# Three stages of a two-block kernel in a new order: the start, the join between output projection and swiglu, and the last stage of attention

## The chip, the cores and the metric

The kernel runs on one core of a Trainium2 chip. The metric is the device time of one execution in microseconds, the median of the runs. TensorE (PE) multiplies; VectorE (DVE), ScalarE (ACT) and GpSimd (POOL) work element by element; SyncE (SP) issues DMAs. Each engine works through its own queue in order and waits at semaphores for the others.

## What is computed

Two transformer blocks on a sequence of 1024 tokens of width 1024, with a context of 256 tokens for the first block. The first block modulates a normed input by vectors made from `c` and `c_ctx` (the "ada" product), mixes tokens (chunked MLP and gated linear attention), and closes with a swiglu. The second has an LRU branch, banded attention, and again a swiglu:

```python
mod = jnp.split((jax.nn.silu(c) @ w_ada[l] + b_ada[l])[:, None, :], N_MOD, axis=-1)
h_lat = _modulate(_rmsnorm(x, norm1_g[l]), sh1, sc1)
h_ctx = _modulate(_rmsnorm(ctx, norm1_g[l]), sh1c, sc1c)
...
x = x + g1 * mix_l
x = x + g2 * _swiglu(_modulate(_rmsnorm(x, norm2_g[l]), sh2, sc2), w_ffn_in[l], w_ffn_out[l])
...
merged = gates[:, :, 0] * y_a + gates[:, :, 1] * y_b
x = x + merged @ w_out[l]
xn2 = rmsnorm(x, norm_ffn_g[l])
gu = xn2 @ w_ffn_in[l]
x = x + (jax.nn.silu(ff_gate) * ff_up) @ w_ffn_out[l]
```

## The kernel before

All data stand transposed: 8 tiles of 128 features, tokens along the free axis, in a context part (256) and two halves (512 each), "half 0" and "half 1". To keep fp32 accuracy every operand is split into a high part (ACT, a copy to fp32r: `s_xh`, `s_wh`) and a low part (DVE, the difference: `s_xl`, `s_wl`), and a product is three matmuls: high by high (L290), low by high (L291), high by low (L292). A *job* is one 128-column tile of a weight by one half: 24 matmuls over 8 tiles k. `products_pe` runs several jobs side by side, k outermost, so that with two jobs each k takes 6 matmuls; `mids` are calls put in ahead of a k.

Weights go through a ring: raw tiles by SP into two buffers `WS` (512 KB each), high parts into four places `WH`, low parts into `WL`. A raw tile is loaded when the tile two before it has its low part, and a place in `WH` is free when the product four tiles before is done. `weights_act`, `weights_dve`, `weights_sp` advance the ring to a given tile, and where they stand in a queue decides when.

The order of each engine is written out by hand, stage by stage, in functions `sp_`, `pe_`, `act_`, `dve_`, `pool_`. The steps that recur:

- An rms norm of a half: ACT squares 8 tiles, DVE or POOL adds them (L1500, L1493), PE sums the columns (`sums_pe`, L1508: 4 matmuls of one column), ACT takes the root, DVE the reciprocal and a diagonal `s_dia` (L1513), PE spreads it to all partitions (`spread_pe`, L1545), DVE scales each tile (L1591), ACT takes the high, DVE the low part.
- Stage 0 (L442 on): the ada product (L570) of 8 row tiles into four banks, the squares and sums of the context and both halves, ACT's copy of the four bank rows (`s_mrow`, L618), 16 transposes of them (L596), the modulated context and half 0. Stage 1 begins with `firsts`: four jobs (al, k0, k1, k2) by context, half 0 and half 1, and half 1 is modulated in between, on DVE after the first jobs' low part (L855).
- `residual_stage("wo", ...)` (L1768): pairs of jobs (p, h) for p in 0 to 3 and h in 0, 1, in that order. After each, DVE adds the gained result to x (tiles `s_lq`, four buffers, loaded by SP) into `s_res`, ACT squares, POOL adds. The norm of half 0 stands in the last pair, that of half 1 at the head of the swiglu.
- `swiglu` (L1877): four plain pairs of jobs (two tiles by two halves; the column sums of half 1 ahead of k = 3, the spread ahead of k = 6 of the first). Then 20 tiles, each as seven products of 12 matmuls (L2126 to L2128) instead of eight: P1, P2, P6, P5, P7, P4, P3. Their inputs are sums of quarters of the normed input: T1, T2, T3 and T4, made once on DVE and ACT (T4 takes the place of half 1's upper tiles); their weights are folded sums S1 to S4 of raw quarters on DVE (L2353 to L2360), with high parts on ACT (L2266) and low parts on DVE (L2367).
- Stage 6 (L3010): 32 units of attention with 16 fill jobs beside them. The last eight multiply half 0 by `wo2` and store the result. Stage 7 (L3300) loads it and x2 back (`s_res`, `s_lq`), adds them to half 0's result, and multiplies half 1 by the same weights in four pairs (`wo2b`), with the norm of half 0 in them.

## Time and profile before

| | us |
|---|---|
| median of 3 runs | 3408.72 |
| lowest and highest | 3406.57 and 3416.22 |
| profiled execution | 3411.13 |
| its span (first to last instruction) | 3409.8 |
| busy: PE, weight loads, DVE, ACT, POOL | 3261.6, 2651.7, 1928.6, 1379.7, 384.0 |

The granted clock of PE was 0.984 of full speed on average. A row of the timeline gives the start and the duration in us, the engine, the line, the operation, what it writes and reads, and in brackets how long the engine had been idle and what released it. Full-speed 128x512 matmuls overlap, so their spacing tells the rate, not their duration.

### The profile page before, as it was taken

Reading aid. Unit: us, or ns where it says so; the run is one execution under the profiler, and the core shown is the slowest. Engines: PE = TensorE matmul, PEld = TensorE weight load, DVE = VectorE, ACT = ScalarE, POOL = GpSimd, SP = SyncE. Lnnn points to the kernel's source line nnn. Section 1 sums busy time; section 2 is a strip of 40 time slices with the busy share of each in tenths; the row PEclk is TensorE's granted clock in tenths of the full one; section 3 lists DMA queues with packets and bytes.
Section 4 is the critical chain, followed back from the end, with each engine's and each line's share of the span. In section 5 each row is a group of like instructions: output and inputs, shape, how many; then the busy total and the mean of one; then the engine's idle time right before and its main releaser. Section 6 shows DMA issues by size and latency. Waiting matters only on the chain. (4 is left out here: it accounts for less than half of the span.)

```text
span 3409.8 us, 39604 instructions
## 1 busy us (share of the span) xinstructions
PE 3261.6 (96%) x14862; PEld 2651.7 (78%) x14862; DVE 1928.6 (57%) x3098; ACT 1379.7 (40%) x2325; POOL 384.0 (11%) x605
## 2 busy tenths in 40 slices
PE   6999999999999999999999999998888799999998
PEld 3888888878888778888888888877556588888886
DVE  4474433456334387777445454664676587777443
ACT  4593222244333243333233355554575343333221
POOL 0121100002100300000011101111211200001011
PEclk8999999999999999999999999999999899999999
DMA  5366444346543323334852434445744523335752
GB/s 220 107 206 197 134 126 135 124 148 224 190 156 99 126 90 118 105 118 150 254 176 81 164 108 148 134 147 164 163 93 105 185 90 121 112 111 170 240 182 75
DMA packets 228045, 494.14 MB, mean 145 GB/s; under 512 B 21520, under 2 KB 84624, under 8 KB 226320
## 3 DMA queue, kind: packets, MB, share of 16 engines
q1 hardware_dynamic: 147728, 302.30, 28.0%
q0 software_dynamic: 80128, 189.30, 17.0%
q8 instruction: 120, 1.97, 0.2%
q14 instruction: 69, 0.57, 0.1%
HBM read 353.63 MB, written 137.89 MB: 144 GB/s over the span
## 5 line engine op out<-in xcount | busy, mean ns | idle before, releaser
L290 PE MATMUL p<-s_xh,s_wh 128*128 128x512 f32 x2256 | 901.6, 400 | 32.9 <-DVE s_tmp L401 12.3
L291 PE MATMUL p<-s_xl,s_wh 128*128 128x512 f32 x2256 | 885.3, 392 | 0.0
L292 PE MATMUL p<-s_xh,s_wl 128*128 128x512 f32 x2256 | 885.2, 392 | 0.0
L290 PEld LDWEIGHTS p<-s_xh,s_wh 128*128 128x128 f32 x2256 | 428.6, 190 | 127.3 <-issue 22.6
L292 PEld LDWEIGHTS p<-s_xh,s_wl 128*128 128x128 f32 x2256 | 427.5, 190 | 91.2
L291 PEld LDWEIGHTS p<-s_xl,s_wh 128*128 128x128 f32 x2256 | 428.4, 190 | 88.8 <-issue 1.7
L2126 PE MATMUL p<-s_xh,s_wh 128*128 128x512 f32 x1152 | 449.5, 390 | 2.1 <-DVE s_xl L2233 1.1
L2128 PE MATMUL p<-s_xh,s_wl 128*128 128x512 f32 x1152 | 448.2, 389 | 0.0
L2127 PE MATMUL p<-s_xl,s_wh 128*128 128x512 f32 x1152 | 448.2, 389 | 0.0
L250 DVE TENSOR_TENSOR s_wl<-s_ws,s_wh 128x1024 fp32r<-128x1024 f32 x157 | 195.3, 1256 | 232.9 <-ACT s_wh L242 232.6
L2126 PEld LDWEIGHTS p<-s_xh,s_wh 128*128 128x128 f32 x1152 | 216.3, 188 | 48.8 <-issue 4.2
L389 ACT ACTIVATE s_tmp<-p 128x512 f32<-128x512 f32 (+1 forms) x125 | 74.3, 594 | 441.0 <-PE p L292 441.0
L2127 PEld LDWEIGHTS p<-s_xl,s_wh 128*128 128x128 f32 x1152 | 216.3, 188 | 45.1 <-issue 0.5
L2128 PEld LDWEIGHTS p<-s_xh,s_wl 128*128 128x128 f32 x1152 | 216.3, 188 | 45.1
L242 ACT ACTIVATE s_wh<-s_ws 128x1024 fp32r<-128x1024 f32 x157 | 162.7, 1049 | 76.5 <-PE p L292 35.3
L2266 ACT ACTIVATE s_wh<-s_ws 128x512 fp32r<-128x512 f32 x148 | 91.9, 625 | 146.7 <-PE p L2128 112.1
L2266 ACT ACTIVATE s_wh<-s_qb 128x512 fp32r<-128x512 f32 x140 | 87.3, 625 | 119.3 <-PE p L2128 111.7
L2477 POOL DMA_DIRECT2D d_h<-s_fhl x80 | 42.6, 533 | 756.6 <-DVE s_fhl L2372 724.0
L2367 DVE TENSOR_TENSOR s_wl<-s_ws,s_wh 128x512 fp32r<-128x512 f32 x148 | 106.4, 731 | 32.5 <-ACT s_wh L2266 32.3
L2367 DVE TENSOR_TENSOR s_wl<-s_qb,s_wh 128x512 fp32r<-128x512 f32 x140 | 100.1, 724 | 37.5 <-ACT s_wh L2266 37.3
L2272 ACT ACTIVATE s_fhl<-s_rb 128x512 fp32r<-128x512 f32 x80 | 50.7, 634 | 141.2 <-DVE s_rb L2410 135.0
L1493 POOL TENSOR_TENSOR s_acc<-s_acc,s_tmp 128x512 f32<-128x512 f32 x49 | 63.7, 1301 | 354.5 <-ACT s_tmp L1486 354.3
(381 smaller groups left out, 5102.4 us busy)
## 6 DMA issues: line engine op xcount, KB each, us to landing
d_h<-s_fhl POOLq DMA_DIRECT2D x80, 512.0 KB, 3.2
s_ws<-i_Wf SPq DMA_DIRECT2D x48, 512.0 KB, 4.3
s_qb<-i_Wf SPq DMA_DIRECT2D x40, 512.0 KB, 4.0
s_qb<-i_Wf SPq DMA_DIRECT2D x80, 256.0 KB, 3.1
s_ws<-i_Wf SPq DMA_DIRECT2D x80, 256.0 KB, 2.9
s_aw<-i_adaT SPq DMA_DIRECT2D x32, 512.0 KB, 3.6
s_xh<-d_h POOLq DMA_DIRECT2D x16, 1024.0 KB, 12.1
s_xl<-d_h POOLq DMA_DIRECT2D x16, 1024.0 KB, 14.8
```

Source lines behind the costliest of these rows:

```text
L242: ac.activation(WH[:, i % NW, 0:n], WS[:, i % NS, 0:n], ACT.Copy).then_inc(*w_hi.up())
L250: dv.tensor_tensor(WL[:, i % NW, 0:n], WS[:, i % NS, 0:n], WH[:, i % NW, 0:n].bitcast(F), ALU.subtract).then_inc(*w_lo.up())
L290: pe.matmul(o, wh, H[:, k, c:c + n], start=(k == 0), stop=False)
L291: pe.matmul(o, wh, L[:, k, c:c + n], start=False, stop=False)
L292: last = pe.matmul(o, wl, H[:, k, c:c + n], start=False, stop=(k == 7))
L389: ac.activation(o, ps, ACT.Copy, scale=p.scale).then_inc(*evA.up())
L1493: po.tensor_tensor(a, a, TMP[:, s.slot, :], ALU.add).then_inc(*sumP.up())
L2126: pe.matmul(o, wh[:, c], H[:, k, :], start=(start and k == 0), stop=False)
L2127: pe.matmul(o, wh[:, c], L[:, k, :], start=False, stop=False)
L2128: x = pe.matmul(o, wl[:, c], H[:, k, :], start=False, stop=(stop and k == 3))
L2266: ac.activation(half_tile(u.slot)[0], u.src, ACT.Copy).then_inc(*u_hi.up())
L2367: dv.tensor_tensor(l, u.src, h.bitcast(F), ALU.subtract).then_inc(*u_lo.up())
```

## The change

1. **Stage 0 and the first products.** Loads: `cc` first, then the ada tiles, with the context, weight tiles 0 to 3 (2 and 3 raw in `ACC` and `RB`) and x in half tiles of 256 KB between them. Squares go to space in `TMP` and to ada tiles that are done with; ACT squares half 0 and half 1 whole, DVE adds the context's and half 0's, POOL half 1's. All four weight tiles are split before the ada product ends. Two bank rows are copied by ACT, two by DVE. The column sums and spreads of both halves stand inside `firsts`, which moved into stage 0; half 1's spread is copied to `s_rb`. The context keys are stored from `ACC`.
2. **`residual_stage`.** The order of pairs is (0,0), (0,1), (1,0), (1,1), (2,0), (3,0), (2,1), (3,1). Half 0's column sum stands ahead of k = 5 of (2,1), its spread ahead of k = 0 of (3,1). In the norm, the results of (2,1) are taken before tile 1, and two weight tiles split before tile 4.
3. **`swiglu`.** Half 1's column sum and spread stand ahead of k = 0 and k = 2 of the second plain pair. The first of the 20 tiles runs P1, P2, P6, P5, P7, P3, P4, and the low parts of its weights are made ahead of those of T2 and T3 where their products come first. T3's sums stand in `RB` instead of `ACC`.
4. **Stages 6 and 7.** Four of the eight `wo2` results are kept in SBUF (`PART`) rather than stored. x2 has eight buffers (`X2`), loaded with the four stored results after the last score product, ahead of further weight tiles. Half 0's column sum and spread stand ahead of k = 2 and k = 6 of the third pair.

```diff
+        def sp_():
+            sp.dma_start(sc2[:], D["cc"]).then_inc(*cc_in.up())
+            for k in range(8):
+                sp.dma_start(AD[:, k, :], D["ada"][k]).then_inc(*ad_in[k].up())
+                if k == 0:
+                    sp.dma_start(XC[:], D["ctxT"]).then_inc(*xc_in.up())
...
+                elif 2 <= k < 6:
+                    weights_sp(k - 1)
+                elif k == 6:
+                    x_sp(0, range(4))
...
+        def pe_():
+            for k in range(8):
+                ada_pe(k)
+                if k == 2:
+                    columns_pe("c")
+                if k == 4:
+                    spread_pe("c")
+            columns_pe(0)
...
+            products_pe(firsts[0], {3: lambda: spread_pe(0)})
+            products_pe(firsts[1], {1: lambda: columns_pe(1), 3: lambda: spread_pe(1)})
+            products_pe(firsts[2])
...
+            for k in range(8):
+                high_act("c", k)
+                if k < 6:
+                    square_act(1, 2 + k)
+            for k in range(2):
+                high_act(0, k)
+            ACW.wait_ge(*w_lo.at(3))
+            for g, p in enumerate(firsts[0][1:]):
+                ACW.wait_ge(*p.mm)
+                ac.activation(ACC[:, 256 * g:256 * g + 256], B[p.bank][:, 0:256], ACT.Copy).then_inc(*evA.up())
+            al_act(0)
+            root_act(1)
...
+            modulated_dve("c", {1: lambda: inverse_dve(0)})
+            modulated_dve(0, {5: lambda: inverse_dve(1)})
+            al_dve(0)
+            modulated_dve(1)
...
+        def pool_():
+            for k in range(1, 8):
+                POW.wait_ge(*squares.at(16 + k + 1))
+                POW.wait_ge(*added1.at(k - 1))
+                po.tensor_tensor(SQ[1][0], SQ[1][0], SQ[1][k], ALU.add).then_inc(*added1.up())
...
-        pairs = plan_pairs(name)
+        pairs = plan_pairs(name, [(0, 0), (0, 1), (1, 0), (1, 1), (2, 0), (3, 0), (2, 1), (3, 1)])
...
-                if p == 3 and h == 1:
-                    products_pe(js, {4: lambda: sums_pe(s0)})
-                    spread_pe(0, DIA[:, 0, :], s0.diag, n0.q[7])
-                else:
-                    products_pe(js)
+                products_pe(js, {5: lambda: sums_pe(s0)} if (p, h) == (2, 1) else {0: lambda: spread_pe(0, DIA[:, 0, :], s0.diag, n0.q[7])} if (p, h) == (3, 1) else None)
...
-                products_pe(e.js, {3: lambda: sums_pe(s1), 6: lambda: spread_pe(1, DIA[:, 1, :], s1.diag, q1[7])} if e is plain[0] else None)
+                products_pe(e.js, {0: lambda: sums_pe(s1), 2: lambda: spread_pe(1, DIA[:, 1, :], s1.diag, q1[7])} if e is plain[1] else None)
...
+        def products_of(p):
+
+            return PRODUCTS if p.n else PRODUCTS[:5] + PRODUCTS[:4:-1]
...
-        items += [("wo2", m, "new first", "plain", dW2, "wo2", 1.0, TC) for m in range(8)]
+        items += [("wo2", m, "new first", "plain", dW2, "wo2", 1.0, TC) for m in range(4)]
+        items += [("wo2", m, "new first", "kept", (PART[:, m, :], sc_mm.at(128)), "wo2", 1.0, TC) for m in range(4, 8)]
...
-            products_pe(pairs[1], {6: lambda: sums_pe(s0)})
-            products_pe(pairs[2], {4: lambda: spread_pe(0, DIA[:, 0, :], s0.diag, n0.q[7])})
+            products_pe(pairs[1])
+            products_pe(pairs[2], {2: lambda: sums_pe(s0), 6: lambda: spread_pe(0, DIA[:, 0, :], s0.diag, n0.q[7])})
```

ACT's queue in the start stage, before: `s_rb`, `s_acc` and `s_tmp` from `s_xc` and `s_res` are squares, `s_rc` the roots, `s_wh` the weights' high parts, `s_mrow` the bank rows.

```order
5 L505 ACTIVATE s_tmp<-s_res 128x512 x10
6 L606 ACT_TABLE_LOAD
7 L606 ACTIVATE s_rc<-p,s_eps 128x2
8 L505 ACTIVATE s_tmp<-s_res 128x512 x4
9 L606 ACTIVATE s_rc<-p,s_eps 128x4 x2
10 L242 ACTIVATE s_wh<-s_ws 128x1024 x2
11 L618 ACTIVATE s_mrow<-p 2x512 x4
12 L242 ACTIVATE s_wh<-s_ws 128x1024 x2
13 L521 ACTIVATE s_ch<-s_tmp,s_modc 128x256 x8
14 L521 ACTIVATE s_xh<-s_tmp,s_mod 128x512 x8
```

The same queue in the change, up to the first context tiles (`s_ch`); the squares now go to `s_ad`.

```order
4 L616 ACTIVATE s_rc<-p,s_eps 128x2
5 L250 ACTIVATE s_wh<-s_ws 128x1024 x2
6 L250 ACTIVATE s_wh<-s_acc 128x1024
7 L250 ACTIVATE s_wh<-s_rb 128x1024
8 L610 ACTIVATE s_ad<-s_res 128x512 x8
9 L640 ACTIVATE s_mrow<-p 2x512 x2
10 L616 ACTIVATE s_rc<-p,s_eps 128x4
11 L610 ACTIVATE s_ad<-s_res 128x512 x2
12 L622 ACTIVATE s_ch<-s_tmp,s_modc 128x256
13 L610 ACTIVATE s_ad<-s_res 128x512
14 L622 ACTIVATE s_ch<-s_tmp,s_modc 128x256
```

The four weight tiles moved ahead of the squares of half 0 and of the bank rows, and squares of half 1 stand between the context tiles.

DVE's queue at the first of the 20 tiles of the first block's swiglu, before, from the last T2 low part: `s_t2l`, `s_t3l` are low parts of T2 and T3, `s_wl` those of the weights, `s_acc` and `s_s` the folded weights, `s_tmp` and `s_fhl` a plain pair's result.

```order
700 L2233 TENSOR_TENSOR s_t2l<-s_lq,s_t2h 128x512 x4
701 L2233 TENSOR_TENSOR s_t3l<-s_acc,s_t3h 128x512 x2
702 L2233 TENSOR_TENSOR s_t3l<-s_s,s_t3h 128x512 x2
703 L2378 TENSOR_TENSOR s_tmp<-p,s_tmp 128x512
704 L2372 TENSOR_TENSOR s_fhl<-s_tmp,s_fhl 128x512
705 L2367 TENSOR_TENSOR s_wl<-s_ws,s_wh 128x512
706 L2353 TENSOR_TENSOR s_acc<-s_ws 128x512
707 L2355 TENSOR_TENSOR s_acc<-s_acc,s_ws 128x512
708 L2367 TENSOR_TENSOR s_wl<-s_ws,s_wh 128x512
709 L2367 TENSOR_TENSOR s_wl<-s_acc,s_wh 128x512
```

And in the change:

```order
703 L2421 TENSOR_TENSOR s_tmp<-p,s_tmp 128x512
704 L2415 TENSOR_TENSOR s_fhl<-s_tmp,s_fhl 128x512
705 L2410 TENSOR_TENSOR s_wl<-s_ws,s_wh 128x512
706 L2395 TENSOR_TENSOR s_acc<-s_ws 128x512
707 L2397 TENSOR_TENSOR s_acc<-s_acc,s_ws 128x512
708 L2410 TENSOR_TENSOR s_wl<-s_ws,s_wh 128x512
709 L2271 TENSOR_TENSOR s_t2l<-s_lq,s_t2h 128x512 x4
710 L2410 TENSOR_TENSOR s_wl<-s_acc,s_wh 128x512 x2
711 L2421 TENSOR_TENSOR s_tmp<-p,s_tmp 128x512
712 L2415 TENSOR_TENSOR s_fhl<-s_tmp,s_fhl 128x512
713 L2271 TENSOR_TENSOR s_t3l<-s_rb,s_t3h 128x512 x2
714 L2271 TENSOR_TENSOR s_t3l<-s_s,s_t3h 128x512 x2
```

The low parts of P1's and P2's weights stand before the eight low parts of T2 and T3, where they stood behind them.

SP's queue at stage 7, before: `s_ws` are weight tiles, `s_lq` x2, `s_res` the stored results (the two alternate eight times).

```order
350 L260 DMA s_ws<-i_Wwo 128x1024 x5
351 L3352 DMA s_lq<-d_x 128x512
352 L3362 DMA s_res<-d_wo 128x512
353 L3352 DMA s_lq<-d_x 128x512
354 L3362 DMA s_res<-d_wo 128x512
```

And in the change (four alternations, then four x2 tiles alone):

```order
351 L269 DMA s_ws<-i_Wwo 128x1024 x3
352 L3397 DMA s_x2half<-d_x 128x512
353 L3406 DMA s_parthalf<-d_wo 128x512
...
360 L3397 DMA s_x2half<-d_x 128x512 x4
361 L269 DMA s_ws<-i_Wwo 128x1024 x2
362 L3397 DMA s_x2half<-d_x 128x512 x8
```

Two of the five weight tiles moved behind the loads of half 0, and those of half 1 stand together.

## Rows read from the trace of the kernel before

**Rows 1.** The page's first part: busy time, share and instructions.
```profile
PE 3261.6 (96%) x14862; PEld 2651.7 (78%) x14862; DVE 1928.6 (57%) x3098; ACT 1379.7 (40%) x2325; POOL 384.0 (11%) x605
```

**Rows 2.** Stretches: busy us, records, granted clock, DMA share, GB/s.
```profile
1300.00:1350.00 50.00, 50.00 (x223) 41.39 (x222) 36.63 (x58) 19.63 (x34) 3.19 (x6) 1.00 0.36 122
1180.00:1190.00 10.00, 7.57 (x26) 5.42 (x25) 5.16 (x8) 3.06 (x5) 0.26 (x1) 0.84 0.00 0
```

**Rows 3.** Timeline of PE at the start: start, duration, operation, idle before.
```profile
7.44 16.81 PE L570 MATMUL p<-s_ad,s_sc 128*2 128x512 f32 x32 [7.44 <-DMA s_ad<-i_ada]
...
40.39 3.60 PE L570 MATMUL p<-s_ad,s_sc 128*2 128x512 f32 x8
...
50.71 0.40 PE L290 MATMUL p<-s_ch,s_wh 128*128 128x256 f32 x1 [3.46 <-DVE s_cl L531]
...
57.27 0.55 PE L290 MATMUL p<-s_ch,s_wh 128*128 128x256 f32 x1 [5.10 <-DVE s_wl L250]
...
81.58 0.76 PE L290 MATMUL p<-s_xh,s_wh 128*128 128x512 f32 x1 [11.32 <-DVE s_al L855]
...
126.57 0.39 PE L292 MATMUL p<-s_xh,s_wl 128*128 128x512 f32 x1
```

**Rows 4.** Timeline at the start: bank rows, turning, first context tile.
```profile
44.02 2.02 ACT L618 ACTIVATE s_mrow<-p 2x512 f32<-2x512 f32 x4 [1.37 <-PE p L570]
...
46.09 1.15 PE L596 MATMUL p<-s_ident,s_mrow 2*128 2x2 f32 x16 [0.20 <-ACT s_mrow L618]
...
49.60 0.89 ACT L521 ACTIVATE s_ch<-s_tmp,s_modc 128x256 fp32r<-128x256 f32 x2
```

**Rows 5.** Timeline of PE at the first block's join.
```profile
1175.58 1.05 PE L1508 MATMUL p<-s_ones,s_acc 128*128 128x1 f32 x8 [1.33 <-POOL s_acc L1493]
...
1187.10 0.47 PE L290 MATMUL p<-s_xh,s_wh 128*128 128x512 f32 x1 [2.43 <-ACT s_xh L1575]
...
1201.66 2.07 PE L1545 MATMUL p<-s_dia,s_ones 128*128 128x512 f32 x2 [3.31 <-DVE s_dia L1513]
...
1240.50 0.47 PE L2126 MATMUL p<-s_xh,s_wh 128*128 128x512 f32 x1 [0.94 <-DVE s_wl L2367]
...
1254.93 0.47 PE L2126 MATMUL p<-s_xh,s_wh 128*128 128x512 f32 x1 [0.55 <-DVE s_xl L2233]
```

**Rows 6.** Timeline of DVE at the same join.
```profile
1203.78 1.41 DVE L2172 SCALAR_TENSOR_TENSOR s_qb<-s_res,s_gs,p 128x512 f32<-128x512 f32 x2 [2.17 <-PE p L1545]
...
1232.86 2.49 DVE L2233 TENSOR_TENSOR s_t2l<-s_lq,s_t2h 128x512 fp32r<-128x512 f32 x4
...
1239.67 0.68 DVE L2367 TENSOR_TENSOR s_wl<-s_ws,s_wh 128x512 fp32r<-128x512 f32 x1
```

**Rows 7.** Timeline of DVE and POOL, an addition of squares beside low parts.
```profile
1187.58 0.74 DVE L1598 SCALAR_TENSOR_TENSOR s_xl<-s_tmp,s_mod,s_xh 128x512 fp32r<-128x512 f32 x1
...
1189.74 1.28 POOL L1493 TENSOR_TENSOR s_acc<-s_acc,s_tmp 128x512 f32<-128x512 f32 x1 [13.72 <-ACT s_tmp L1486]
...
1190.22 1.35 DVE L1598 SCALAR_TENSOR_TENSOR s_xl<-s_tmp,s_mod,s_xh 128x512 fp32r<-128x512 f32 x1
```

**Rows 8.** Timeline of PE at the second block's join.
```profile
2643.90 0.50 PE L290 MATMUL p<-s_xh,s_wh 128*128 128x512 f32 x1
...
2677.78 1.87 PE L1508 MATMUL p<-s_ones,s_acc 128*128 128x1 f32 x8 [9.07 <-DVE s_acc L1500]
...
2713.88 0.77 PE L290 MATMUL p<-s_xh,s_wh 128*128 128x512 f32 x1 [6.78 <-DVE s_wl L250]
...
2725.72 1.86 PE L1508 MATMUL p<-s_ones,s_acc 128*128 128x1 f32 x8 [6.16 <-POOL s_acc L1493]
...
2783.92 0.47 PE L2126 MATMUL p<-s_xh,s_wh 128*128 128x512 f32 x1 [0.54 <-DVE s_xl L2233]
```

**Rows 9.** Timeline of DVE at the second block's join.
```profile
2734.05 1.41 DVE L2172 SCALAR_TENSOR_TENSOR s_qb<-s_res,s_vec,p 128x512 f32<-128x512 f32 x2 [5.23 <-PE p L1545]
...
2768.67 0.68 DVE L2367 TENSOR_TENSOR s_wl<-s_ws,s_wh 128x512 fp32r<-128x512 f32 x1
```

More of the change, by code:

```diff
@@ L378, in fill_act @@
             ac.activation(VF[p.vq][:, 0:p.n], ps, ACT.Copy).then_inc(*evA.up())
+            return
+        if p.kind == "kept":
+            out, free = p.dst
+            ACW.wait_ge(*free)
+            ac.activation(out, ps, ACT.Copy).then_inc(*evA.up())
             return
@@ L555, in stage0 @@
[L555 removed]
+        column_bank, spread_bank = {"c": 6, 0: 6, 1: 3}, {"c": 4, 0: 5, 1: 3}
         scale_of = {"c": GS[:, 8:16], 0: GS[:, 0:8], 1: GS[:, 0:8]}
         shift_of = {"c": MODC, 0: MOD, 1: MOD}
[L559 to L564 removed]
@@ new lines, in ada_pe, with columns_pe @@
+        def ada_pe(k):
+            PEW.wait_ge(*silu.at(1))
+            PEW.wait_ge(*ad_in[k].at(1))
+            for c in range(4):
+                last = pe.matmul(B[c][0:2, :], sc2[:, k, :], AD[:, k, c * 512:c * 512 + 512], start=(k == 0), stop=(k == 7))
+            last.then_inc(*ada.up())
+        def columns_pe(what):
+            PEW.wait_ge(*{"c": added.at(7), 0: added.at(14), 1: added1.at(7)}[what])
+            PEW.wait_ge(*const.at(1))
+            if what == 1:
+                PEW.wait_ge(*spread3_free)
+            for j in range(size[what] // 128):
+                c = 4 * which[what] + j
+                last = pe.matmul(B[column_bank[what]][:, c:c + 1], SQ[what][0][:, 128 * j:128 * j + 128], ones[:, 0:1], start=True, stop=True)
+            last.then_inc(*colsum.up())
@@ new lines, in high_act, with al_act @@
+        def high_act(what, k):
+            s, c, H, L, c0 = dst[what]
+            n, q = size[what], which[what] * 8 + k
+            ACW.wait_ge(*shifted.at(q + 1))
+            ac.activation(H[:, k, c0:c0 + n], TMP[:, q % NT, 0:n], ACT.Identity, bias=shift_of[what][:, k:k + 1]).then_inc(*x_hi.up())
+        def al_act(part):
+            p = firsts[part][0]
+            ACW.wait_ge(*p.mm)
+            ac.activation(AL[:, p.col:p.col + p.n], B[p.bank][:, 0:p.n], ACT.Copy).then_inc(*al_hi.up())
@@ new lines, in al_dve, with square_dve @@
+        def al_dve(part):
+            p = firsts[part][0]
+            lo = AL[32:64, p.col:p.col + p.n]
+            DVW.wait_ge(*al_hi.at(part + 1))
+            dv.tensor_tensor(lo, B[p.bank][32:64, 0:p.n], lo.bitcast(F), ALU.subtract).then_inc(*al_lo.up())
+        def square_dve(what, k):
+            n = 8 * which[what] + k
+            DVW.wait_ge(*squares.at(n + 1))
+            DVW.wait_ge(*added.now())
+            dv.tensor_tensor(SQ[what][0], SQ[what][0], SQ[what][k], ALU.add).then_inc(*added.up())
@@ new lines, in stage0, with done @@
+        sp_()
+        pe_()
+        act_()
+        dve_()
+        pool_()
+        low_rank = al_hi, al_lo, wal_hi, wal_lo, cm_in, cb_silu, [x_lo.at(24), ctx_out.at(3)]
+        gone = [spread.at(3), shifted.at(24)]
+        p0.close()
+        def done():
+            retire(cc_in, xc_in, *x_in.values(), *ad_in, wal_in, cm_in, cb_in, silu, ada, squares, added, added1, colsum, rooted, recip, diag, spread, spread_copied,
+                   mcopy, mcopy_d, mturn, mods, shifted, al_hi, al_lo, wal_hi, wal_lo, cb_silu, ctx_out)
@@ L3294, in stage6 @@
         done.gone, done.scores, done.y0 = ended(), sc_mm.at(128), jobs[-1].mm
+        done.x2, done.part, done.parts = X2, PART, [p.ev for p in jobs[12:]]
         retire(*key_in, *q_in, *zb_in, *mb_in, v_in, ad_in, padded, negated, sc_mm, biased, sink_d, exps, divided, turned, copied, weighed, gated, merged,
@@ L3328, in stage7 @@
             f = Plan()
-            f.m, f.part, f.done = m, part_in[m % 4].due(), summed.due()
-            f.q, f.free, f.arrived = plan_gate(f.done)
+            f.m, f.done = m, summed.due()
             ready[(m, 0)] = f.done
```

649 lines of the change are left out of this document (302 added, 347 removed).

## The prediction

> **What bounds the kernel.** I read the granted clock and the 40 slices first, then PE's waits, then the timeline around each wait. PE is busy 96% of the span [rows 1]: TensorE is the bound, and time can come only from its waits, from stretches at half clock, and from work taken away. The change takes no product away. At full rate one 128x512 product costs 0.226 us: the 50 us in [rows 2] hold 223 records, and as one lasts longer than the next one's start, two of them began before: 50 / 221. So a pair of jobs (48 products) is 10.9 us, three of the four-pass groups of one half (96) are 21.8, and one of the seven products (12) is 2.72. In the same row DVE is busy 36.6 of 50: it has slack in the steady part, and only there.
>
> PE waits in three places that the change touches: the start, until 126.6 [rows 3]; the join of the first block's wo stage with its swiglu [rows 5]; and the same join in the second block [rows 8]. Attention between them waits too, but its order stays.
>
> **The start.** Before: the ada products end at 43.99 (40.39 + 3.60), the first real product starts at 50.71, the next is held 5.10 us for weights, the first full half is held 11.32 us, and the last product of the three parts starts at 126.57 [rows 3].
> Now the ada tiles go first, x and weights are slotted between. Ada runs 16.81 + 4 x 3.60 [rows 3], plus two column sums and a spread between them, some 1.6 us by the 1.05 us for eight records and the 2.07 us at half clock of the like in [rows 5]: 32.8 us. The first tile should land 0.6 us earlier, as two small loads no longer stand ahead: 6.8 + 32.8 = 39.6. Transfers are no longer the limit there (the sum of the loads ahead of the last ada tile falls by one tile's worth, and the engine is later than they are). Two bank rows are copied by ACT (0.5 each, a quarter of 2.02 [rows 4]) and two by DVE, whose copy of this shape no row shows: between 0.4 and 1.0 each, I take 0.7. So 41.0, turning 1.15 [rows 4], 42.2. Before, 3.5 us lay between the end of the turning and the first product, of which 1.3 were ACT's two weight copies ahead of the first context tile (s_ch at 49.60 [rows 4]); these are now done earlier: 42.2 + 2.15 = 44.35, against 50.71. All four weight tiles are split by then, so the 5.10 us wait goes.
> What is late next is the feeding of the context part. DVE needs 0.4 + 0.45 us for a tile and ACT alternates with squares, about 1 us for a step. But the second half's seven additions of squares now go to POOL at that moment, 1.28 us each, and [rows 7] show a DVE operation of 0.74 us taking 1.35 when such an addition runs. So I take 1.28 + 0.48 = 1.76 us for a step while seven of them run: 44.35 + 0.9 (the diagonal of half 0) + 12.3 + 1.4 for the last step's products = 59.0, where PE at full clock alone would be done at about 56, and with the half clock after the idle time at 58.
> The Trainium skill, "SBUF — State Buffer", section "Who interferes with whom", has the rule: a DVE operation with two SBUF inputs and a GpSimd operation that reads SBUF exclude each other for a whole instruction. The trace agrees (0.74 to 1.35). By a view in which they run side by side, the sum would be 1 to 2 us better.
> From there: 1 us until half 0's first tile is split (60.5 with the copies of the context banks), then two halves of 21.8, a column sum 0.9, a spread 1.0 and 0.3 of waiting for its diagonal: 106.3. Half 1 is ready at about 84, when it is needed, since its spread copy is made at 72. The end of the last product's slot moves from 126.8 to 106.3: **20.5 us**. The 3 us of weight wait behind it stay. Bounds: 24 if the steps take 1 us and the clock holds; 14 if half clock lasts through the whole context part (+4) and the evictions behind two half-0 tiles on ACT delay the second column sum by 2 to 3 more.
>
> **First join.** Before, the last pair of wo starts at 1168.7 (the wait at 1175.58 began after 24 products). The half-0 norm cannot start until its column sum in that pair, so the next products wait until 1187.10, and the other half's diagonal is waited for 3.31 us at 1201.66 [rows 5]. Now pair (3,0) runs ahead of (2,1): half 0 is complete 10.9 us earlier, its sums stand in (2,1), its spread opens (3,1), and norm and two weight tiles (4 x 1.3 us before they are met) are done under (3,1). The swiglu's first pair of jobs starts at 1168.7 + 0.9 + 1.0 + 10.9 = 1181.5. x loads: four buffers, loaded two pairs ahead, so they hide. The second column sum now opens the second pair of jobs: 1192.4; its squares, with DVE's queue and two POOL additions, are complete at about 1192.3, and the weight low parts of that pair at 1192.6 and 1194.4, so 0.5 us is lost. DVE starts the half-1 norm at 1181.5 + 10.9 + 0.9 + 2.7 + 1.0 + 0.1 + 0.5 = 1197.6, against 1203.78 [rows 6]. The four jobs end at 1181.5 + 43.5 + 1.9 + 0.5 = 1227.4, against 1239.6: 12 us gained.
> Then DVE is the bound. From 1203.78 to the low part of the first unit at 1239.67 it worked through [rows 6]: 35.9 us. The eight T2 and T3 low parts (8 x 0.60, 2.49 for four [rows 6]) now stand behind, so 31.1: the unit's low part at 1228.7, P1 at +0.83 = 1229.5, PE waits 2.1. From there to P4's low part the queue holds 33 operations of 0.60 and four round trips over ACT of 0.7 to 0.8, 22.9 us, and P4 now needs all four T4 low parts and its own behind them: P4 starts at 1228.7 + 23.1 = 1251.8, where six products need only 16.3. So the first pair loses some 6 us inside (about 1 at P7, 5 at P4), and ends at 1254.5. Before, P4 began at 1254.93 and P3 followed: 1254.93 + 2 x 2.72 = 1260.4. Gain 5.9 less one spell of half clock behind the 5 us wait: the stretch behind a wait of 2.43 us shows a clock of 0.84 over 10 us [rows 2], that is 3.2 us at half rate, 1.6 lost. **4.3 us**. Bounds: 8 if DVE is 3 us less in debt, 0 if two spells come and the 2.1 us wait brings one too.
>
> **Second join.** The last fill job starts at 2643.90 [rows 8], so wo2b's first pair at 2649.4. Before, x2 and the stored halves were loaded behind two weight tiles and through four buffers; the sums stood 9.07 us in PE's way at 2677.78, then weights 6.78 at 2713.88, sums again 6.16 at 2725.72, and P4 started at 2783.92 [rows 8]. Now half of the parts stay in SBUF, twelve loads go out from about 2647 in one go (3 MB; 122 GB/s at a DMA share of 0.36 [rows 2] is some 340 at full, so 9 us), and DVE, free at 2651.6, finds them. Weights and additions for half 0 end at 2669.7; its sum stands at 2673.8, its spread at 2680.2. Pairs 0 to 3 end at 2649.4 + 43.5 + 1.9 = 2694.8. The first swiglu weights come after the norm tiles and their ACT copies: low parts at 2696.5 and 2697.6, a wait of 2.2: effective start 2697.0. The second sum now opens the second pair of jobs, so half-1 norm starts 15.6 later, at 2712.6, against 2734.05 [rows 9]. There the way to the first unit's low part (2768.67) was 34.6, less 4.8: 2742.4; P1 waits 0.8; P4 at +23.1 = 2765.5; end 2768.2. Before 2783.92 + 5.44 = 2789.4. Gain 21.2 less 1.6 for half clock: **19.5 us**. Bounds: 24 with no new spell and the earlier POOL additions out of the way; 14 if the twelve loads slow the last fill's stores and weights and half 0's sum misses its place.
>
> **Neutral edits.** t3 moved from s_acc to s_rb adds no operation, only a wait that DVE's order meets; the stage 1 buffers move without a new wait; four stores fewer. From P1 of the second pair on, everything is as before and PE-bound.
>
> **Sum.** 20.5 + 4.3 + 19.5 = 44.3. The profiled execution took 3411.1, so 3366.8 for it; the median of the runs is 2.4 lower: **3364 us**, 1.3% less. The bounds of the three terms give 28 to 56 off, thus 3353 to 3381 around it.
>
> **Rivals.** (a) The start is worth only half: ACT holds the context banks behind two half-0 tiles and their eviction holds the second column sum, with half clock all through. For: ACT's queue is strictly in order and so full there. Against: each hold is 1 to 3 us by the rows. 3374. (b) The joints: DVE, which already carries 36.6 of 50, is late at both first pairs and every join takes two or three spells of half clock: 3 us more at each join and the 2 us waits doubled: 3377. (c) Better: DVE's copies and POOL's additions interfere little and the first pair's T4 chain is met sooner: 3352. (d) The change doesn't do what it says: the early sums are not early, since loads or DVE delay half 0 in both stages, and only the start and 5 us remain: 3386 to 3400. (e) Slower: DVE stays behind after the first pair. The first pair ends with DVE's queue full, its low parts only 1.5 to 2 us ahead of PE; if a pair's work on DVE with its trips over ACT took more than 19.0 us, the debt would never shrink, and 1.5 us for each of 39 further pairs would be 59: 3423. It decides when DVE's share goes over 50 of 50; it is 36.6 [rows 2], so it should win back 5 us for each pair.
>
> **Numbers.** Forecast 0.66, (a) 0.10, (b) 0.08, (c) 0.08, (d) 0.05, (e) 0.03. The range must take in the forecast's own 3353 to 3381 with (c) and (b): 3351 to 3383. About 0.3% (10 us) can be told from no change: faster 0.93, within 0.04, slower 0.03.
>
> **What would show it.** PE's first real product at 44 to 45 and the end of the three parts near 106; a DVE operation of two SBUF inputs at 1.0 us or more beside POOL's seven additions; no wait on s_res, s_acc or s_dia over 1 us at the joins; a new wait of 4 to 6 us on a low part at the seventh product of both first pairs, and a small one at the first; behind it no wait. Wrong would be: a wait at the first join's second pair of jobs over 2 us, a second column sum in the start stage that PE waits for, or waits recurring pair by pair.

## The result, and the profile after

| us | before | changed |
|---|---|---|
| median (four runs each) | 3407.64 | 3372.84 |
| lowest and highest | 3404.79, 3416.22 | 3367.57, 3376.60 |
| profiled execution, its span | 3411.13, 3409.8 | 3367.57, 3366.3 |

The ratio of the means is 0.9893, with an interval of 0.9868 to 0.9917: 36 us less (the medians differ by 34.8). The forecast was 3364 in a range of 3351 to 3383. The profiled execution of the changed kernel is its fastest run and came out at 3367.6, where the sum had said 3366.8. It will be seen below that this closeness is partly luck.

The first part of the page of the changed kernel, beside [rows 1]: PE is less busy by 9 us only, at the same number of instructions, the other 34 us of span were its waits.

```profile
PE 3252.2 (97%) x14862; PEld 2646.6 (79%) x14862; DVE 1929.7 (57%) x3093; ACT 1378.3 (41%) x2324; POOL 390.9 (12%) x608
```

PE's timeline at the start of the changed kernel, beside [rows 3]: the first context product, half 0's spread, half 1's column sum and spread, and the first wait behind the three parts.

```profile
44.85 0.55 PE L299 MATMUL p<-s_ch,s_wh 128*128 128x256 f32 x1 [3.16 <-DVE s_cl L695]
51.41 1.02 PE L585 MATMUL p<-s_ad,s_ones 128*128 128x512 f32 x2
62.21 0.95 PE L580 MATMUL p<-s_ones,s_ad 128*128 128x1 f32 x8
68.60 1.02 PE L585 MATMUL p<-s_ad,s_ones 128*128 128x512 f32 x2
...
108.11 0.36 PE L299 MATMUL p<-s_ch,s_wh 128*128 128x256 f32 x1 [3.08 <-DVE s_wl L258]
```

The first product started at 44.85 (forecast 44.35), and the sum and the spread of half 1 were met without a wait. The three parts end where the last wait begins: 108.11 - 3.08 = 105.03, against 129.94 - 2.98 = 126.96 before. That is 21.9 us, where 20.5 was forecast.

PE's waits at the first join, beside [rows 5], and then at the second, beside [rows 8]:

```profile
1200.77 0.47 PE L2160 MATMUL p<-s_xh,s_wh 128*128 128x512 f32 x1 [2.02 <-DVE s_wl L2410]
1223.22 0.77 PE L2160 MATMUL p<-s_xh,s_wh 128*128 128x512 f32 x1 [4.24 <-DVE s_xl L2271]
...
2653.77 2.08 PE L1578 MATMUL p<-s_dia,s_ones 128*128 128x512 f32 x2 [4.06 <-DVE s_dia L1546]
2717.59 0.47 PE L2160 MATMUL p<-s_xh,s_wh 128*128 128x512 f32 x1 [0.72 <-DVE s_wl L2410]
2729.72 0.47 PE L2160 MATMUL p<-s_t3h,s_wh 128*128 128x512 f32 x1 [0.96 <-ACT s_wh L2310]
2740.04 0.77 PE L2160 MATMUL p<-s_xh,s_wh 128*128 128x512 f32 x1 [4.62 <-DVE s_xl L2271]
```

At the first join the two waits are those of the forecast, P1's 2.02 us (2.1) and P4's 4.24 (5); the one of about 1 us at P7 is missing in this execution. At the second, P1 0.72 (0.8), P7 0.96 (1) and P4 4.62 (5) are as forecast too. The first of its rows was not: the spread of half 0 waits 4.06 us for its diagonal, where the prediction wanted no wait on `s_dia` over 1 us.

To say where time went I cut each trace at five landmarks that every kernel here has: A, the first product of queries and keys of the gated attention (start and interleaved stage 1 lie before it); B, the last turning in the token mixing; C, the column sum at the end of the first swiglu; D, the last turning of probabilities in the banded attention; E, the first column sum in the closing phase of the second swiglu. B to C holds the first join, D to E the second. From E to the last column sum it is 102.85 us (once 102.86) in every kernel that shows both; in one kernel (no_sw) E is taken as that sum less 102.85.

| us | to A | A to B | B to C | C to D | D to E |
|---|---|---|---|---|---|
| before | 397.40 | 481.71 | 886.29 | 870.54 | 658.50 |
| changed | 369.42 | 480.99 | 883.51 | 871.19 | 644.97 |
| changed, again | 372.07 | 481.40 | 882.74 | 873.64 | 647.82 |
| root_first | 371.24 | 480.89 | 882.11 | 873.12 | 645.07 |
| p4_first | 373.47 | 482.24 | 881.00 | 873.88 | 644.39 |
| lows_late | 374.91 | 481.49 | 881.70 | 875.08 | 647.02 |
| sp_root | 370.95 | 482.24 | 883.37 | 871.32 | 638.72 |
| no_start | 395.50 | 482.09 | 882.13 | 877.36 | 647.08 |
| no_sw | 374.22 | 481.59 | 883.89 | 870.24 | 639.49 |
| no_s7 | 370.81 | 480.90 | 882.07 | 872.92 | 658.84 |
| no_res | 371.15 | 482.23 | 888.01 | 870.20 | 645.96 |
| joined | 373.59 | 480.89 | 881.04 | 870.93 | 633.89 |
| joined_filled | 373.12 | 481.58 | 878.86 | 870.80 | 630.92 |
| adds_on_dve | 374.90 | 481.68 | 882.20 | 870.22 | 647.95 |

The columns also show what one execution can't tell: the stretch to A takes 369.4 to 374.9 us in the twelve traces whose start is the changed one (in adds_on_dve but for seven additions), and C to D 870.2 to 877.4 in all fourteen, though almost nothing differs there. The trace of the changed kernel is the best of the twelve in the first and in the middle in the second.

C to D moves with the time that PE spent at the lower of its two granted clocks (1.2 GHz, half of the full 2.4): that was 34.1 us in the six traces between 870.2 and 871.2, 37.5 in the four between 870.9 and 873.1, 41 in the three between 873.6 and 875.1, and 44.4 in no_start, at 877.4. Against the kernel before, no_start has 10.3 us more of it there, which at half rate is 5 of its 7 us, and 2 us more of waits (58.4 in sum for 56.4). Up to A (the record of the clock begins 11 to 13 us after the start) the kernel before spent 27.3 us at the lower clock, the changed kernel 6.8 in its first trace and up to 13.7 in the others.

### The profile page after: what moved, and what is told of

Its sections match the earlier page's. It is cut to its first block and busy times, and to the rows that moved or that the text cites. A ratio compares the mean times of both kernels' runs of the same rounds, so it can differ in the third digit from the quotient of the medians.

```text
span 3366.3 us, 39597 instructions
## 1 busy us (share of the span) xinstructions
PE 3252.2 (97%) x14862; PEld 2646.6 (79%) x14862; DVE 1929.7 (57%) x3093; ACT 1378.3 (41%) x2324; POOL 390.9 (12%) x608
## 3 DMA queue, kind: packets, MB, share of 16 engines
q8 instruction: 120, 1.97, 0.2%
## 5 line engine op out<-in xcount | busy, mean ns | idle before, releaser
L299 PE MATMUL p<-s_xh,s_wh 128*128 128x512 f32 x2256 | 899.1, 399 | 12.5 <-DVE s_tmp L417 12.3
L2160 PEld LDWEIGHTS p<-s_xh,s_wh 128*128 128x128 f32 x1152 | 217.9, 189 | 59.0 <-issue 13.7
```

Source lines behind the costliest of these rows:

```text
L299: pe.matmul(o, wh, H[:, k, c:c + n], start=(k == 0), stop=False)
L2160: pe.matmul(o, wh[:, c], H[:, k, :], start=(start and k == 0), stop=False)
```

## The experiments

Times are medians of four to six runs, four kernels on one chip at a time, with the kernel before beside them (its medians: 3407.6 to 3409.6). For the changed kernel I take the median of its eight runs in two places, 3372.9.

### The changed kernel again

> The changed kernel once more, as the base for the runs beside it. By my account of its trace it saves 43.5 us of span in the profiled execution, but the median of its four runs is 5 us above that execution, and they fall in two groups (3367.6, 3369.6 and 3376.1, 3376.6). If the groups are a property of the kernel (some wait that is met in one execution and missed in the next), they show again and the median is 3368 to 3377. If the second group was chance of one chip, all runs are within 3 us of 3369. Either way waits: P4's product of the first pair 4.2 us at the first join and 4.6 at the second, the spread of half 0 in the last stage 4.1 us.

Measured: 3372.93 us (3367.66 to 3374.98), ratio 0.9893 (0.9878 to 0.9908). The runs lie spread between 3367 and 3377, in no two groups. P4's wait at the second join was 4.62 again, the diagonal's 5.67 instead of 4.06. The median is 5 us above the execution that I had explained. This second trace, 7 us above it, is longer to A by 2.7 us, C to D by 2.5, and D to E, where the diagonal is, by 2.9.

### The parts undone one by one

no_start is the changed kernel with stages 0 and 1 of before; no_res has the old order of pairs:

```diff
-        pairs = plan_pairs(name, [(0, 0), (0, 1), (1, 0), (1, 1), (2, 0), (3, 0), (2, 1), (3, 1)])
+        pairs = plan_pairs(name)
```

(and half 0's sum, spread and norm where they stood); no_sw has the whole swiglu of before, no_s7 stages 6 and 7 of before.

> The changed kernel with stages 0 and 1 of the kernel before. By my sum it loses the start's 21 to 22 us: first decay-block product (the first after the interleaved stage) back from 369 to 375 to some 393 to 397, the time 3393 to 3395. If the 5 us that the profiled execution won in addition in stage 1 belong to the start's rewriting, it loses 26 to 28 and comes to 3399; if they are chance of the transfers of the ada rows, 3394.

Measured: 3394.89 us, 22.0 above the changed kernel, as forecast. To A it took 395.5.

> The changed kernel with the old order of pairs in wo, (2,0), (2,1), (3,0), (3,1), half 0's sum and spread in the last pair; the new swiglu behind it. The three other parts undone so far were worth 22 (start), 8 (last stage) and minus 7.5 us (swiglu), 22.5 of the 36 that the whole change gave. If the parts add up, this one carries the remaining 13: 3386. By my forecast's mechanism (half 0's norm starts a pair earlier, the swiglu's first pair 12 us earlier, but DVE's chain behind it holds the first pair of seven products), the chain gets most of it back: DVE's norm of half 1 would start 8 to 10 us later than now, and P4's wait of 4.2 stays: 3380 to 3383.

Measured: 3377.47 us, 4.6 above; B to C 888.0 instead of 882.1 to 883.5. PE's waits at the first join:

```profile
1149.11 1.05 PE L1541 MATMUL p<-s_ones,s_acc 128*128 128x1 f32 x8 [0.58 <-POOL s_acc L1526]
1159.04 0.47 PE L299 MATMUL p<-s_xh,s_wh 128*128 128x512 f32 x1 [2.43 <-ACT s_xh L1608]
1163.64 0.47 PE L299 MATMUL p<-s_xh,s_wh 128*128 128x512 f32 x1 [1.59 <-DVE s_xl L1631]
```

The old 2.43 us behind the spread is back, and P1 and P4 wait 1.97 and 4.59 as well. Both expectations were higher, 3380 to 3383 and 3386. The parts do not add up to 36: 22.0 + 4.6 + 8.4 - 7.5 (below) = 27.5. What is missing lies between the last two.

> The changed kernel with stages 6 and 7 of before: all eight results stored and loaded back, x2 through four buffers, half 0's sum at k = 6 of the second pair, while the swiglu behind it has the new order. By my account of the traces the last stage and its join gave 13.5 us: last score to end of the second swiglu back from 645 to 648 us to some 657 to 660, the time 3384 to 3387. The forecast's own term, 19.5, would give 3392.

Measured: 3381.3 us, 8.4 above, 3 less than expected; D to E 658.8, as expected. PE's waits in the last stage are those of [rows 8], 9.26 for the sum and 6.63 for the swiglu's first weights. The third one there, for half 1's sum, is gone, but P4 waits 4.62 instead, and D to E is no shorter than before (658.5):

```profile
2648.73 1.87 PE L1534 MATMUL p<-s_ones,s_acc 128*128 128x1 f32 x8 [9.26 <-DVE s_acc L1526]
2684.97 0.76 PE L299 MATMUL p<-s_xh,s_wh 128*128 128x512 f32 x1 [6.63 <-DVE s_wl L258]
```

> The changed kernel with the swiglu of before: half 1's column sum and spread in the first plain pair, eight T2 and T3 low parts first, P4 ahead of P3. By the two runs on the order (P4 first was faster by 1 to 2 us at each join, late low parts the same within 1), only the place of the sum can count: at the first join it stands at k = 3, where the squares are complete 5 us later, so PE waits 4 to 5 there, but DVE starts its norm at the same time as now; at the second it is met at once and DVE starts 5 us earlier. So: within 3 us of the changed kernel, rather faster, 3368 to 3374. The rival, that this part carries the gain at the joins: 3378 or more.

Measured: 3365.44 us (3360.58 to 3366.1), ratio 0.9864 (0.9849 to 0.988): without its third part the change is 7.5 us faster, more than I had expected (3368 to 3374). PE's waits at the two joins:

```profile
1168.67 1.87 PE L1541 MATMUL p<-s_ones,s_acc 128*128 128x1 f32 x8 [6.34 <-POOL s_acc L1526]
1214.82 0.47 PE L2156 MATMUL p<-s_xh,s_wh 128*128 128x512 f32 x1 [1.36 <-DVE s_wl L2397]
...
2660.37 2.07 PE L1578 MATMUL p<-s_dia,s_ones 128*128 128x512 f32 x2 [5.12 <-DVE s_dia L1546]
...
2682.89 1.05 PE L1541 MATMUL p<-s_ones,s_acc 128*128 128x1 f32 x8 [0.68 <-POOL s_acc L1526]
...
2738.95 0.47 PE L2156 MATMUL p<-s_xh,s_wh 128*128 128x512 f32 x1 [0.58 <-DVE s_xl L2263]
```

At the first join the early column sum costs a wait of 6.34 us and saves P4's, and B to C is the same within 1.8. At the second half 0's diagonal is waited for as in the changed kernel, but the squares of half 1 are complete in time; the sum waits 0.68, no product later waits over 0.6, and D to E is 639.5. So the new last stage is worth 658.5 - 639.5 = 19.0 us with the old swiglu behind it, and 12 with the new one.

### The order in the first pair

p4_first puts P4 back ahead of P3; lows_late puts the low parts of T2 and T3 back ahead of the weights'.

```diff
 # p4_first
-            return PRODUCTS if p.n else PRODUCTS[:5] + PRODUCTS[:4:-1]
+            return PRODUCTS
...
+            fold_dve(6)
             low_dve(6)
 # lows_late, on DVE; ACT's high parts likewise
+            second_low_dve()
+            third_low_dve()
             plain_dve(plain[2])
             low_dve(0)
             fold_dve(2)
             low_dve(1)
-            second_low_dve()
             low_dve(2)
             low_dve(3)
             plain_dve(plain[3])
-            third_low_dve()
```

> P3 still ahead of P4, but the eight low parts of T2 and T3 stand ahead of the first weights' low parts again, on ACT the T2 and T3 high parts likewise. Theory A (DVE is the bound until P4's input is made, whatever its order): P1 waits some 4.8 us more (6 to 7 us instead of 2.0 at the first join, 5 to 6 instead of 0.7 at the second), P4's wait falls by the same to under 1 us, and the time is that of the changed kernel within 2 us. Theory B (early products are worth what they start earlier): 8 to 10 us slower.

Measured: 3372.11 us. P1 waits 6.80 and 5.51, P4 no longer waits, and the time is the same: theory A holds, with its numbers.

```profile
1211.59 0.76 PE L2160 MATMUL p<-s_xh,s_wh 128*128 128x512 f32 x1 [6.80 <-DVE s_wl L2408]
...
2733.42 0.77 PE L2160 MATMUL p<-s_xh,s_wh 128*128 128x512 f32 x1 [5.51 <-DVE s_wl L2408]
```

> The first pair of seven products in the old order, P4 ahead of P3, everything else as changed; S4 is folded ahead of P3's low part as before. Theory A (DVE-bound first pair): P4 waits 2.7 us more in each of the two swiglus, 6.5 to 7.5 us, and P3 comes behind it, so each loses the 2.1 us that a product beside the wait had hidden, less a fold and a low part: 3 to 5 us slower than the changed kernel in sum. Theory B (the order is without effect, since P3's own weights come as late): 0 to 1 us.

Measured: 3369.31 us, ratio 0.9885 (0.987 to 0.9899), 3.6 below the changed kernel where 3 to 5 above was expected. Between two medians that is not certain, but the traces agree: P4 waits 3.09 and 3.45 us, where 6.5 to 7.5 was expected. DVE's low parts at the second join, first of the changed kernel, then of p4_first:

```profile
2729.42 0.68 DVE L2403 TENSOR_TENSOR s_s<-s_ws,s_acc 128x512 f32<-128x512 f32 x1
2730.81 0.69 DVE L2410 TENSOR_TENSOR s_wl<-s_s,s_wh 128x512 fp32r<-128x512 f32 x1 [0.70 <-ACT s_wh L2310]
...
2736.74 2.49 DVE L2271 TENSOR_TENSOR s_xl<-s_lq,s_xh 128x512 fp32r<-128x512 f32 x4
2739.14 0.68 DVE L2410 TENSOR_TENSOR s_wl<-s_ws,s_wh 128x512 fp32r<-128x512 f32 x1
```

```profile
2736.13 0.68 DVE L2410 TENSOR_TENSOR s_wl<-s_ws,s_wh 128x512 fp32r<-128x512 f32 x1
...
2742.04 2.49 DVE L2271 TENSOR_TENSOR s_xl<-s_lq,s_xh 128x512 fp32r<-128x512 f32 x4
```

With P3 ahead, its fold (S4), a trip over ACT and its low part stand ahead of T4's sums, and P4's own weight comes behind all four T4 low parts (2739.14). With P4 ahead its weight is ready (2736.13), and P4 begins at 2742.87, behind the first T4 low part only. From P1's start to P4's it is 2742.87 - 2724.30 = 18.57 us, against 2740.04 - 2717.59 = 22.45. The product that P3 hides is 2.72 us, the chain is 3.9 shorter: 1.2 us for P4 first, at each join (at the first the two lengths are 18.57 and 22.45 as well). I had counted the first and not the second. Of the 3.6 us these are 2.4; the rest is within what the other stretches differ by.

### What held the diagonal

In the changed kernel, ACT's queue at half 0's root, and SP's ahead of it:

```profile
2648.73 1.06 ACT L250 ACTIVATE s_wh<-s_ws 128x1024 fp32r<-128x1024 f32 x1 [4.62 <-DMA s_ws<-i_Wwo]
2650.14 1.06 ACT L250 ACTIVATE s_wh<-s_ws 128x1024 fp32r<-128x1024 f32 x1 [0.36 <-DMA s_ws<-i_Wwo]
2651.22 1.28 ACT L1563 ACT_TABLE_LOAD   x1
2652.51 0.26 ACT L1563 ACTIVATE s_rc<-p,s_eps 128x4 f32<-128x4 f32 x1
```

```profile
2624.99 16.22 SPq L3397 DMA_DIRECT2D s_x2half<-d_x  x8
2641.24 1.01 SPq L269 DMA_DIRECT2D s_ws<-i_Wwo  x2
```

The column sum starts at 2643.16, but the root stands behind two weight tiles. These are asked for at 2641.24, because the eight x2 tiles of half 1 stand ahead of them on SP, and each waits until DVE has added the tile of half 0 in the same place. root_first moves the root (and on DVE the diagonal) ahead of the weights; sp_root also moves the request:

```diff
 # root_first, on ACT; on DVE likewise
+            sums_act(s0)
             weights_act(ahead(pairs[2][0].i, 2))
-            sums_act(s0)
 # sp_root in addition
                 residual_sp(m, 1)
+                if m == 3:
+                    weights_sp(ahead(pairs[1][0].i, 2) + NS)
```

> In the last stage the root and the diagonal of half 0 stand ahead of the third pair of weight tiles on ACT and DVE, not behind. Theory A (the 4.06 us wait for the diagonal comes from ACT's queue: it holds the root behind two weight tiles whose DMA was issued late): the wait falls below 0.3 us, and the half clock behind it goes too, so 6 to 7.5 us less than the changed kernel; but DVE then starts the norm of half 1 by as much earlier, so the later waits stay as they are. Theory B (the join is bound by DVE from half 0's norm to the first pair, so that whatever is won ahead is waited for at P4): the gain is under 2 us and P4's wait grows from 4.6 to 8 or more.

Measured: 3371.8 us, 1.1 below: the time of theory B, the mechanism of neither. The wait for the diagonal is gone, P4's is 4.59 as before, and a new one of 4.95 us stands at the swiglu's first weights. PE's rows, and DVE's queue behind the diagonal:

```profile
2651.80 1.02 PE L1578 MATMUL p<-s_dia,s_ones 128*128 128x512 f32 x2
...
2671.41 0.77 PE L299 MATMUL p<-s_xh,s_wh 128*128 128x512 f32 x1 [4.95 <-DVE s_wl L258]
```

```profile
2648.89 0.69 DVE L1546 TENSOR_TENSOR s_dia<-s_ident,s_rc 128x512 f32<-128x512 f32 x1
2652.34 1.22 DVE L258 TENSOR_TENSOR s_wl<-s_ws,s_wh 128x1024 fp32r<-128x1024 f32 x1 [2.76 <-ACT s_wh L250]
2654.39 1.23 DVE L258 TENSOR_TENSOR s_wl<-s_ws,s_wh 128x1024 fp32r<-128x1024 f32 x1 [0.82 <-ACT s_wh L250]
```

The late tiles now hold DVE ahead of the norm of half 0, and the norm holds the swiglu's weights.

> As root_first, and on SP the two weight tiles of the last wo2b pair are asked for behind the fourth of the eight x2 tiles of half 1, not behind all eight. Theory A (root_first only moved the wait: DVE stood at low parts of weights whose transfer was asked for at 2644, behind tiles that are not needed yet): the transfer goes out at once when its buffer is free, some 4.6 us earlier, and has 1 MB less ahead of it; neither the diagonal's wait (4 to 6 us) nor root_first's new one at the swiglu's first weights (4.95) is there, and last score to end of the second swiglu falls from 645 to 648 us to 640 or 641. Theory B (P4 collects it all): P4's wait of 4.6 grows by 4 and that stretch stays at 644 or more.

Measured: 3367.62 us (3363.27 to 3368.8), ratio 0.9875 (0.9858 to 0.9892); D to E 638.7, theory A and a little more (640 or 641). SP asks at 2637.36, and of the 4.95 us there remain 1.02; P4's wait did not grow:

```profile
2637.36 2.68 SPq L269 DMA_DIRECT2D s_ws<-i_Wwo  x2
2640.32 3.93 SPq L3397 DMA_DIRECT2D s_x2half<-d_x  x4
```

```profile
2668.01 0.47 PE L299 MATMUL p<-s_xh,s_wh 128*128 128x512 f32 x1 [1.02 <-DVE s_wl L258]
...
2737.25 0.77 PE L2160 MATMUL p<-s_xh,s_wh 128*128 128x512 f32 x1 [4.62 <-DVE s_xl L2271]
```

### A faster version

```diff
 # joined: sp_root and p4_first, and
+                at, when = (plain[1], (0, 2)) if shift else (plain[0], (4, 7))
 # joined_filled in addition
-            plain_dve(plain[2])
+            plain_dve(plain[2], lambda: fold_dve(2))
...
-            plain_dve(plain[3])
+            plain_dve(plain[3], lambda: second_low_dve(range(3, 4)))
             third_low_dve()
-            for i in range(4, 6):
-                fold_dve(i)
-                low_dve(i)
-            for k in range(4):
+            fold_dve(4)
+            combine_third_dve(0)
+            low_dve(4)
+            low_dve(5)
+            for k in range(1, 4):
                 combine_third_dve(k)
```

(`shift` is set in the first block only; `at` is the plain pair in which half 1's sum and spread stand, `when` their k. The call that `plain_dve` takes stands between its two operations.)

> Three corrections together: root and transfer order of sp_root, P4 ahead of P3 again, and at the second join alone half 1's column sum ahead of k = 4 and its spread ahead of k = 7 of the first plain pair (the squares are complete there; at the first join they are not, so it stays). Theory A (at both joins the chain on DVE from half 1's diagonal to T4's low parts sets P4, so what counts is when that chain starts and how long it is): the chain starts 4 to 6 us earlier at the second join, P4's wait there goes from 4.6 to under 1, at the first join from 4.3 to 3.1: last score to end of the second swiglu 632 to 635 us (638.7 in sp_root), the time 3359 to 3361. Theory B (other waits take their place): 3365 or more.

Measured: 3357.56 us (3356.67 to 3359.96), ratio 0.9853 (0.984 to 0.9866); D to E 633.9, B to C 881.0. P4 waits 3.49 us at the first join (3.1 expected) and 1.60 at the second (under 1). D to E is 4.8 less than in sp_root, of which P4 first is 1.2; by subtraction the earlier sum and spread are worth the other 3.6.

> As joined, and DVE's 0.7 us round trips over ACT in that chain are filled: S1 and S2 folded between a plain pair's product and its low part, a T2 low part in the next, a T4 sum in the one behind S3. Three trips of 0.7 us less per chain: at the first join P4's wait falls from 3.1 to some 1.0 and the spell of half clock behind it may go: 2 to 4 us less than joined, 3356 to 3358. If the chain is not DVE's own length but ACT's, nothing: 3360.

Measured: 3352.61 us (3346.96 to 3355.94), ratio 0.9834 (0.9821 to 0.9848), 20 us below the changed kernel and 5 below joined, where 2 to 4 was expected. PE's waits in the first pairs of joined_filled:

```profile
1205.61 0.47 PE L2160 MATMUL p<-s_xh,s_wh 128*128 128x512 f32 x1 [2.52 <-DVE s_wl L2411]
1221.47 0.47 PE L2160 MATMUL p<-s_xh,s_wh 128*128 128x512 f32 x1 [1.97 <-DVE s_xl L2272]
...
2727.49 0.47 PE L2160 MATMUL p<-s_xh,s_wh 128*128 128x512 f32 x1 [0.50 <-DVE s_wl L2411]
```

At the first join P4 waits 1.97 instead of joined's 3.49 (1.0 expected; P1 0.5 more, as S1 and S2 now stand ahead of its weights), B to C is 2.2 less; in the second block's nothing waits over 0.5 (the swiglu's first weights ahead of it still cost 1.10), D to E is 3.0 less.

### The additions at the start

> The changed kernel with the seven additions of half 1's squares on DVE, one behind each context tile, instead of on POOL. In the trace of the changed kernel six of the eight context low parts took 1.11 to 1.36 us instead of 0.47 while POOL added, 4.6 us in sum. Theory A (they exclude each other, so POOL's help is no help): seven DVE additions of 128x512 cost 7 x 0.60 = 4.2 us, the low parts are 0.47 again, the context part ends within 0.5 us of where it does (about 59) and half 1's column sum stands at 62 as before; the time is that of the changed kernel. Theory B (the stretching is something else, the clock or the scalar operand): the low parts stay above 1 us and the context part ends 4 us later, the time 3376.

Measured: 3368.96 us, with runs from 3363 to 3374: the time tells nothing. The trace does. DVE's and POOL's rows at the context tiles, changed kernel and then adds_on_dve:

```profile
42.02 1.07 DVE L743 SCALAR_TENSOR_TENSOR s_gs<-s_mod,s_vec 128x8 f32<-128x8 f32 x1
...
46.97 1.11 DVE L695 SCALAR_TENSOR_TENSOR s_cl<-s_tmp,s_modc,s_ch 128x256 fp32r<-128x256 f32 x1
48.40 1.36 DVE L695 SCALAR_TENSOR_TENSOR s_cl<-s_tmp,s_modc,s_ch 128x256 fp32r<-128x256 f32 x1
49.68 0.47 DVE L705 SCALAR_TENSOR_TENSOR s_tmp<-s_xc,s_gs,p 128x256 f32<-128x256 f32 x1
...
41.81 1.26 POOL L760 TENSOR_TENSOR s_ad<-s_ad 128x512 f32<-128x512 f32 x1 [41.37 <-ACT s_ad L610]
...
48.19 2.72 POOL L760 TENSOR_TENSOR s_ad<-s_ad 128x512 f32<-128x512 f32 x2 [0.39 <-ACT s_ad L610]
```

```profile
46.56 0.48 DVE L695 SCALAR_TENSOR_TENSOR s_cl<-s_tmp,s_modc,s_ch 128x256 fp32r<-128x256 f32 x1
46.96 0.69 DVE L727 TENSOR_TENSOR s_ad<-s_ad 128x512 f32<-128x512 f32 x1
```

Without POOL's additions the low part takes 0.48 us, and half 1's column sum stands at 61.16 instead of 61.95 to 62.94 in the eleven kernels with POOL's. So theory A holds: POOL's help is worth nothing here, or minus 1 us. (Stretched are five of the eight low parts, not six; the sixth long operation is half 0's diagonal, 1.78 us, and 0.69 in adds_on_dve.)

The 1 us is lost ahead of the context tiles. POOL's first addition ends at 43.07, and a small operation of DVE (L743), 0.17 us long in adds_on_dve, takes 1.07 beside it and ends at 43.09. So the first product stands at 44.85 here and at 43.55 there; from it to half 1's column sum it is 17.4 to 18.1 us with POOL's additions and 17.6 without.

The low parts have two inputs in SBUF; the scaling of a tile (L705), one of whose inputs is the spread in PSUM, took 0.47 us beside POOL too (49.68). The Trainium skill ("SBUF — State Buffer", section "Who interferes with whom") has both cases: two SBUF inputs contend with a GpSimd operation that reads SBUF, at most one does not. Both rows agree.

## The forecast, step by step

- **What bounds the kernel**: right. The time came from PE's waits (34 of the 43.5 us of span) and from products at the lower clock (9, the number of products being the same), and an edit that only moved waits (lows_late) changed nothing.
- **The start**, forecast 20.5: right, 21.9 in the trace and 22.0 by no_start. The step of 1.76 us by which I priced POOL's interference was 1.4 to 1.7 us in the trace (46.97 to 48.40, for one, is 1.43). The profiled execution won another 6 us up to A, which I hadn't forecast: 28.0 against 21.9 at the end of the three parts. Behind that point the kernel before had two spells at the lower clock, 3.4 us each, and this execution none. Over the twelve kernels with this start the mean to A is 372.5, which is 23.0 less than no_start and 24.9 less than before, so 1 to 3 us of it last. The rest did not come again; I take it for that execution's chance.
- **First join**, forecast 4.3: right in size (2.8 in the profiled execution, 2.8 to 4.2 over the kernels that have it unchanged) and in its two waits. In the profiled execution two spells of half clock came instead of one, one behind each wait, as the lower bound had it. That was not the rule: of the seven traces with this join unchanged the five with one spell gained 3.5 to 4.2, the two with two spells 2.8 and 2.9. The granted clock of the changed kernel at the two waits, and at the two large ones of the second join:

```profile
1200.00:1210.00 10.00, 9.23 (x34) 7.47 (x35) 9.27 (x17) 6.66 (x13) 1.06 (x2) 0.83 0.39 152
1220.00:1230.00 10.00, 6.78 (x17) 5.43 (x18) 9.97 (x17) 5.09 (x9) 0.00 (x0) 0.66 0.19 54
2650.00:2660.00 10.00, 6.23 (x14) 4.24 (x14) 8.41 (x12) 5.67 (x8) 3.56 (x4) 0.66 0.47 161
2740.00:2750.00 10.00, 9.96 (x34) 8.05 (x35) 9.35 (x16) 4.08 (x7) 0.00 (x0) 0.75 0.20 56
```

  (Columns: stretch, its length, busy us of PE, PEld, DVE, ACT and POOL, granted clock, DMA share, GB/s.)
- **Second join**, forecast 19.5 with bounds 14 to 24: the step that failed. D to E fell by 13.5 in the profiled execution and by 10.5 to 12.5 in the others with this code. What I wrote was that twelve loads go out in one go, that half 0's "sum stands at 2673.8, its spread at 2680.2", and that pairs 0 to 3 run through. I had followed the loads of half 0 and not the eight of half 1 behind them, each of which waits, and with them the weight tiles, behind which the root stood on ACT. Counted from landmark D, the sum came when forecast (38.05 us for 37.9), the spread 4.4 late (48.66 for 44.3), and P4 5.4 late (134.93 for 129.6). With the order mended (sp_root) the spread is at 44.45 and P4 at 129.37, and the stretch is 19.8 us shorter than before: the rest of the step was sound.
- **The order of the first pair**, whose gain I had inside the joins' terms: wrong in sign. The low parts' place is worth nothing, P3 ahead of P4 costs about 1.2 us at each join, and the later column sum about 3.6 us at the second (joined against sp_root). I had taken "the second sum now opens the second pair" as settled by its first join, where the squares are late, and never asked whether it had to be so late at the second.
- **From the profiled execution to the median.** The sum agreed with the profiled execution to 1 us because the start gave 7.5 more (28.0 for 20.5) and the joints 7.5 less (2.8 + 13.5 for 4.3 + 19.5). The median is 5 us above that execution. In the second trace the excess lies about equally in three stretches: to A and C to D, whose length the change doesn't explain, and D to E, where the diagonal's wait was 1.6 us longer. So the forecast's 3364 is 9 us below the median, inside its range, and of its three terms only the second join's was clearly too large.
- **The rivals**: (a) has the time nearest to the median, 3374, but not its mechanism: the start was worth its whole term. (b) did not come: the waits at P1 were not doubled, and its 3377 is 2 to 3 us more than its own terms give. Of (d), the late start of half 0's norm did come at the second join, but as 4 to 6 us, and half 0's sum itself was early. (e) did not come: no wait recurs behind the first pair. Of (c), interference was not small (low parts of 1.11 to 1.36 us), and P4's chain was met sooner only in p4_first's order.
- **The signs**: all came but one. The first product, the end of the three parts, the stretched operations and the waits on low parts were as said; the wait on `s_dia` was not, and it pointed at the step that failed.
